# Nineteen weight slots instead of fifteen in the expert stage of a transformer layer, paid for with single row buffers and a residual that is stored and read back

## What is computed

```python
h = rms_norm(x, p['g_pre_ffn']) * (1 + sc) + sh
xb = t[tok_b]
hb = jax.nn.silu(xb @ w1[e]) * (xb @ w3[e])
return (hb @ w2[e]) * w_b[:, None]
...
return x + gt * rms_norm(hierarchical_moe(h, p), p['g_post_ffn'])
```

## Time and profile before

| | |
|---|---|
| median of 3 runs | 1144.94 us (1143.33 to 1145.46) |
| the profiled execution | 1144.4 us, of which the span of the trace is 1142.7 us |
| TensorE busy | 1004.3 us, 88% of the span |
| VectorE, ScalarE, GpSimd busy | 355.0, 280.8, 138.3 us |
| DMA queue of SP | 271.07 MB, 60.5% of the 16 engines' span |
| HBM read, written | 283.34 MB, 25.33 MB |

### The profile page before, as it was taken

How to read it: one execution, slowest core, us unless ns; L and a number is a source line. 1 busy time by engine, 2 the same in 40 slices (tenths; PEclk the granted TensorE clock), 3 DMA queues, 4 the chain that set the end, 5 groups by cost and what they waited for, 6 DMA issues and landing times. The chain is left out here.

```text
span 1142.7 us, 13820 instructions
## 1 busy us (share of the span) xinstructions
PE 1004.3 (88%) x5483; PEld 606.3 (53%) x5483; DVE 355.0 (31%) x633; ACT 280.8 (25%) x533; POOL 138.3 (12%) x219
## 2 busy tenths in 40 slices
PE   4999999999988898999968997799999978588776
PEld 2677778777766787887854332233333322122222
DVE  3553133110388885462392110000000000000006
ACT  4233213222377664022341000000011000000004
POOL 2122221000111301100122000000001000000000
PEclk9899999999989999999997998899999998889999
DMA  9734436444350212633458999999999999999973
GB/s 350 254 113 160 126 110 226 160 168 177 123 184 1 77 55 66 230 129 93 184 202 283 369 401 420 421 422 421 421 420 420 421 419 419 419 416 413 416 312 135
DMA packets 73334, 301.55 MB, mean 264 GB/s; under 512 B 8055, under 2 KB 14328, under 8 KB 48050
## 3 DMA queue, kind: packets, MB, share of 16 engines
q1 hardware_dynamic: 62064, 271.07, 60.5%
q0 software_dynamic: 11040, 29.49, 7.6%
q10 hardware_dynamic: 162, 0.05, 0.0%
HBM read 283.34 MB, written 25.33 MB: 270 GB/s over the span
## 5 line engine op out<-in xcount | busy, mean ns | idle before, releaser
L1387 PE MATMUL psum<-w_hi,act_hi 128*128 128x512 f32 (+1 forms) x480 | 188.6, 393 | 2.8 <-ACT rows L1174 1.4
L1389 PE MATMUL psum<-w_hi,act_lo 128*128 128x512 f32 (+1 forms) x480 | 183.9, 383 | 0.0
L1388 PE MATMUL psum<-w_lo,act_hi 128*128 128x512 f32 (+1 forms) x480 | 183.7, 383 | 0.0
L1782 PE MATMUL psum<-weights_ring,expert_x_columns 128*64 128x512 f32 (+1 forms) x584 | 125.3, 634 | 29.5 <-DMA weights_ring<-in_w_e 18.5
L1320 ACT ACTIVATE expert_y<-psum 128x512 f32<-128x512 f32 x18 | 10.8, 597 | 455.3 <-PE psum L1793 455.3
L1782 PE MATMUL psum<-rows_ring,expert_x_columns 128*64 128x512 f32 (+1 forms) x448 | 103.6, 611 | 9.5 <-DMA rows_ring<-in_w_e 5.9
L1387 PEld LDWEIGHTS psum<-w_hi,act_hi 128*128 128x128 f32 x480 | 90.9, 189 | 32.4 <-issue 14.2
L1389 PEld LDWEIGHTS psum<-w_hi,act_lo 128*128 128x128 f32 x480 | 90.9, 189 | 18.2
L1388 PEld LDWEIGHTS psum<-w_lo,act_hi 128*128 128x128 f32 x480 | 91.1, 190 | 16.3
L1911 DVE TENSOR_TENSOR w_lo<-raw_mix,w_hi 128x2048 fp32r<-128x2048 f32 (+1 forms) x24 | 52.8, 2202 | 148.1 <-ACT w_hi L1069 148.1
L1782 PEld LDWEIGHTS psum<-weights_ring,expert_x_columns 128*64 128x64 f32 (+1 forms) x584 | 37.5, 136 | 103.5 <-issue 102.3
(11 more groups left out here) (345 smaller groups left out, 1275.2 us busy)
## 6 DMA issues: line engine op xcount, KB each, us to landing
weights_ring<-in_w_e SPq DMA_DIRECT2D x78, 1024.0 KB, 28.1
rows_ring<-in_w_e SPq DMA_DIRECT2D x75, 1024.0 KB, 28.5
raw_mix<-in_w_e SPq DMA_DIRECT2D x39, 1024.0 KB, 27.7
raw_mix<-in_w_in SPq DMA_DIRECT2D x16, 1024.0 KB, 5.8
raw_mix<-in_w_ada SPq DMA_DIRECT2D x16, 1024.0 KB, 7.1
ada_first<-in_w_ada SPq DMA_DIRECT2D x8, 1024.0 KB, 14.3
gates_scratch<-rows POOLq DMA_DIRECT2D x20, 256.0 KB, 3.3
y_scratch<-lam SPq DMA_DIRECT2D x1, 5120.0 KB, 16.8
```

What stands on the lines that cost most here:

```text
L1387: pe.matmul(out, a_hi(ka_), w_hi[:, kw, :], start=s, stop=False)
L1388: pe.matmul(out, a_hi(ka_), w_lo[:, kw, :], start=False, stop=False)
L1389: ins = pe.matmul(out, a_lo(ka_), w_hi[:, kw, :], start=False, stop=e)
L1782: ins = pe.matmul(out[x * w:(x + 1) * w, :], expert_xT[:, a:a + w], ring(slots[x % len(slots)])[:, kk * 512:(kk + 1) * 512], start=(k == 0 ...
```

## The change

The ring has 19 slots. Four more are gained by laying the rows ring over 80 KB per partition that end at the tile `pt`. These lie over x1 too, so x1 is stored to HBM (`x1_d`) and read back at the end into ring slots, half a slot per tile (`x1_back`). `xg` and `ysb` have one half instead of two, and the gather of pass p then waits for the transposes of pass p-1, the copy of pass p's result for the scatter of pass p-1. The loads are sorted so that the 12 of passes 0 and 1 go first, and loads 9 to 12 are issued singly, each as its slot comes free.

```diff
-RAW_MIX, RING, HL = 3, 15, 3
+RAW_MIX, RING, HL = 3, 19, 3
...
+    loads.sort(key=lambda x: x[1] >= LEAD)
+    return units, loads + [(len(units), len(passes), 0, i, 0) for i in range(NT + (NT + 1) // 2)]
...
+        xg = at("expert_rows", D, offset=late_base + 2 * D * 4)
+        ysb = at("expert_y", D, offset=late_base + 3 * D * 4)
...
+        rows_ring_base = pt_base - (RING - RAW_MIX - 2 * HL) * UNIT * 4
...
+            x = [9, 0, 6, 7, 1, 2, 8, 5, 4, 3][slot - RAW_MIX - 2 * HL]
...
+        def x1_back(i):
+            return ring((PAIR_LOAD + NT + i // 2) % RING)[:, i % 2 * D:(i % 2 + 1) * D]
...
             def load_pair(i):
                 sp.dma_start(raw_pair(i), y_d[2 * P * i:2 * P * (i + 1), :].rearrange("(p k) n -> p (k n)", k=2)).then_inc(x_in[i], 16)
+                sp.dma_start(x1_back(i), x1_d[i * P:(i + 1) * P, :]).then_inc(x_in[i], 16)
...
                     ring_load(RAW_MIX + 2 * x + 1)
+                    if x == 0:
+                        ring_load(9)
+                ring_load(10)
+                for i in range(NT):
+                    if i == NT - 1:
+                        sp.wait_ge(mix_done, 6 * NT)
+                        ring_load(11)
+                    sp.wait_ge(x1_done, i + 1)
+                    sp.dma_start(x1_d[i * P:(i + 1) * P, :], xrow[:, i, :]).then_inc(h2_out, 16)
                 for i in range(NT):
                     sp.wait_ge(h2_done, i + 1)
                     sp.dma_start(h2_d[i * P:(i + 1) * P, :], yr[:, i, :]).then_inc(h2_out, 16)
-                sp.wait_ge(h2_out, 16 * NT)
+                sp.wait_ge(h2_part, NT)
+                ring_load(12)
+                sp.wait_ge(h2_out, 32 * NT)
                 sp.wait_ge(h2t_done, 2 * NT)
...
             def first_part(i, again):
-                ac.wait_ge(x_in[i], 32 + 16 * again)
+                ac.wait_ge(x_in[i], 48 + 32 * again)
...
-                ve.scalar_tensor_tensor(raw_pair(i)[:, 0:D], raw_pair(i)[:, D:2 * D], stat[:, 8 + i:9 + i], xrow[:, i, :], ALU.mult, ALU.add).then_inc(c_out, 1)
+                ve.scalar_tensor_tensor(raw_pair(i)[:, 0:D], raw_pair(i)[:, D:2 * D], stat[:, 8 + i:9 + i], x1_back(i), ALU.mult, ALU.add).then_inc(c_out, 1)
```

More of the change, by code:

```diff
@@ L106, in expert_units @@
     loads = [(n, p, m, u, x) for n, (p, m, u) in enumerate(units) for x in range(len(passes[p]))]
-    return units, loads + [(len(units), len(passes), 0, i, 0) for i in range(NT)]
+    loads.sort(key=lambda x: x[1] >= LEAD)
+    return units, loads + [(len(units), len(passes), 0, i, 0) for i in range(NT + (NT + 1) // 2)]
 def build(nc, t):
@@ L264, in build @@
         idx_s = at("scatter_column", 2, U32)
-        rbase = [late_base + 4 * D * 4]
+        rbase = [late_base + 3 * D * 4]
         def rb(name, cols, dt=F32):
@@ L270, in rb @@
             rbase[0] += (cols * (2 if dt == BF16 else 4) + 31) // 32 * 32
-            assert rbase[0] <= late_base + 6 * D * 4
+            assert rbase[0] <= late_base + 4 * D * 4 + FE * 4
             return a
-        kbase = [late_base + 7 * D * 4 + FE * 4]
+        kbase = [late_base + 5 * D * 4 + FE * 4]
         def kept(name, cols, dt=F32):
@@ L278, in kept @@
             kbase[0] += (cols * (2 if dt == BF16 else 4) + 31) // 32 * 32
-            assert kbase[0] <= late_base + 2 * KD * TOK * 4
+            assert kbase[0] <= rows_ring_base
             return a
@@ L336, in ring @@
                 return weights_ring[:, x * UNIT:(x + 1) * UNIT]
-            x = slot - RAW_MIX - 2 * HL
+            x = [9, 0, 6, 7, 1, 2, 8, 5, 4, 3][slot - RAW_MIX - 2 * HL]
             return rows_ring[:, x * UNIT:(x + 1) * UNIT]
@@ L475, in build @@
         h2_done = sem("h2_rows_done")
-        h2_out = sem("h2_stored")
+        h2_out = sem("x1_and_h2_stored")
         h2t_done = sem("h2_transposed")
@@ L754, in all_experts @@
                     sp.dma_start(h2_d[i * P:(i + 1) * P, :], yr[:, i, :]).then_inc(h2_out, 16)
-                sp.wait_ge(h2_out, 16 * NT)
+                sp.wait_ge(h2_part, NT)
+                ring_load(12)
+                sp.wait_ge(h2_out, 32 * NT)
                 sp.wait_ge(h2t_done, 2 * NT)
-                for j in range(RAW_MIX + 2 * HL, len(moe_loads)):
-                    if j == RAW_MIX + 2 * HL + 4:
-                        sp.wait_ge(moe_g[0], 16)
-                    if j == RING - 1:
-                        sp.wait_ge(rt_mm, 1 + NT)
+                for j in range(13, len(moe_loads)):
                     ring_load(j)
@@ L771, in pairs @@
             def pairs(again):
+                if not again:
+                    sp.wait_ge(moe_mm, moe_loads[PAIR_LOAD + NT + (NT - 1) // 2 - RING][0] + 1)
+                    sp.wait_ge(all_scattered, 1)
                 for i in range(NT):
-                    if again:
-                        load_pair(i)
+                    load_pair(i)
                 for i in range(NT):
@@ L965, in _ @@
             last_row, last_pair = po.to_reg(TOK - 1), po.to_reg(2 * TOK - 1)
-            po.wait_ge(h2_out, 16 * NT)
+            po.wait_ge(h2_out, 32 * NT)
             def gather(p):
-                if p >= 2:
-                    po.wait_ge(moe_xt, p - 1)
+                if p >= 1:
+                    po.wait_ge(moe_xt, p)
                 if p == LEAD:
@@ L998, in _ @@
             gather(0)
-            gather(1)
             po.wait_ge(tile_mm, 5 * NS)
@@ L1005, in _ @@
             po.dma_start(wk_d.rearrange("(t p k) o -> p t (k o)", p=P, k=2), wk[:, :].rearrange("p (t k) -> p t k", k=2)).then_inc(g2_in, 16)
+            gather(1)
             for p in range(NP - 1):
@@ L1039, in _ @@
                 for i in range(NT):
-                    po.wait_ge(x_in[i], 32)
+                    po.wait_ge(x_in[i], 48)
                 scatter(NP - 1)
@@ L1317, in y_half @@
                 ac.wait_ge(moe_mm, unit_end(p, 2, 1))
-                if p >= 2:
-                    ac.wait_ge(moe_sc[par], 16 * (p // 2))
-                ac.activation(ysb[:, par * D:par * D + 512], bank(5), ACT.Copy).then_inc(moe_ya, 1)
+                if p:
+                    ac.wait_ge(moe_sc[1 - par], 16 * ((p + 1) // 2))
+                ac.activation(ysb[:, 0:512], bank(5), ACT.Copy).then_inc(moe_ya, 1)
             def first_part(i, again):
-                ac.wait_ge(x_in[i], 32 + 16 * again)
+                ac.wait_ge(x_in[i], 48 + 32 * again)
                 if not again and i == 0:
@@ L1814, in transpose_x @@
                     pe.wait_ge(moe_xc, p)
-                rows_transposed(p % 2).then_inc(moe_xt, 1)
+                rows_transposed().then_inc(moe_xt, 1)
             def pair_rows(i):
@@ L1860, in _ @@
                 for x in range(2):
-                    pe.matmul(bank(SUM_BANK[i] + x), loh[:, i * P:(i + 1) * P], ysb[:, LAST_PAR * D + x * 512:LAST_PAR * D + x * 512 + 512], start=True, stop=False)
+                    pe.matmul(bank(SUM_BANK[i] + x), loh[:, i * P:(i + 1) * P], ysb[:, x * 512:x * 512 + 512], start=True, stop=False)
                 pair_rows(i)
@@ L2376, in y_half @@
                 ve.wait_ge(moe_mm, unit_end(p, 2, 1))
-                if p >= 2:
-                    ve.wait_ge(moe_sc[par], 16 * (p // 2))
-                ve.tensor_copy(ysb[:, par * D + 512:(par + 1) * D], bank(6)).then_inc(moe_yv, 1)
+                if p:
+                    ve.wait_ge(moe_sc[1 - par], 16 * ((p + 1) // 2))
+                ve.tensor_copy(ysb[:, 512:D], bank(6)).then_inc(moe_yv, 1)
             ve.wait_ge(pass_mm, 3)
@@ L2386, in pair_sum @@
             def pair_sum(i, again):
[L2387 removed]
+                ve.wait_ge(x_in[i], 48 + 32 * again)
                 ve.wait_ge(c_part, NT * again + i + 1)
```

34 lines of the change are left out of this document (14 added, 20 removed).

## The result

| | us, median (lowest to highest) | executions |
|---|---|---|
| before | 1143.85 (1142.05 to 1145.46) | 10 |
| changed | 1150.09 (1146.92 to 1154.33) | 10 |

The ratio is 1.0053, 95% interval 1.0040 to 1.0067: slower by half a per cent, clear of the spread, and outside the forecast range of 1141.8 to 1149.5 us. The profiled execution took 1150.62 us, its span is 1148.7 us.

What follows compares the result with a forecast made beforehand. The expert stage was taken as bound by weight transfers, the end by the last weight load's landing and the tail: -4.5 + 5.2 = +0.7 us, 1145.1 us profiled, 1145.6 us on the median, range 1141.8 to 1149.5 us.

Steps and rivals of the forecast that it cites:

- Part 2: Tail: x1 read back alternately with the result pairs delays the fourth tile's first part by 5.2 us (5.0 to 6.0).
- The spacing: Tail: one result pair plus its x1 transfer lands every 3.7 to 4.0 us.
- `first_part(4)` adds nothing: Tail: the last tile's data land 18.9 us after the last weight load; ScalarE arrives at 18.8 us, so no added delay.
- Three loads are worth 7.5 us: Front, at load 29's issue: three loads outstanding before, an empty queue now, a gain of 7.5 us before refilling costs.
- I take 4.5 us: Front: both queues full after load 30, so the last weight load lands 4.5 us earlier (4.2 to 5.1).
- The filling: Front: with an empty queue load 29 lands 4.9 us after issue instead of 2.5 us, costing 2.4 us.
- Load 30: Front: the load after 29 lands at 671.3 us instead of 675.5 to 677.6 us, at least 4.2 us gained.
- Hidden by 0.4 us at worst: Front: the second gather lands at 615.8 to 620.5 us, before TensorE wants its rows at 620.9 us; no cost.
- TensorE starts late: Rival, front: late h2 stores or second gather delay TensorE 2 to 4 us, giving 1147.6 to 1149.6 us; chance 0.25.
- The front gains nothing: Rival, front: load 29 late or engines slow for another reason, only the tail's loss left, 1150.1 us; chance 0.08.
- load 29 waits for the same unit of TensorE in both kernels: Front: load 29 reuses the slot of the same weight half in both kernels, so is issued at 662.9 us in both.
- my bound of 600.8 us: Front: the last h2 store lands at most 6.5 us later, at 600.8 us, hidden by 1.2 us before the first gather.

Runs made afterwards that it cites:

- the kernel before with the trip of x1: The kernel before, its slots, load order and buffers kept, with x1 stored and read back alternating with the result pairs: 1149.71 us, ratio 1.0045.
- unit order: The changed kernel with ring slots taken by later loads in the order in which TensorE's units free them: 1141.25 us, ratio 0.9988.
- the early gather: The changed kernel with the second gather issued right behind the first, ahead of the small transfers: 1146.54 us, ratio 1.0023.

## Why the prediction was wrong

**Tail: the mechanism was right, the size off.** Part 2 had 5.2 us, at most 6.0 us; it measured 6.2 us in the changed kernel and 6.3 us alone. The spacing was right (3.70 us, forecast 3.7 to 4.0) and `pair_root(0)` came 5.1 us later against L. The missing term is what the idle stretch does to TensorE: 5.7 us without work, then products at half the clock, 1.1 us at the end. Its size varies with how long the low clock lasts. In the five profiles with the alternation the two groups of four products behind the idle stretch took 3.58 + 1.88, 3.78 + 2.12, 3.78 + 1.94, 3.78 + 2.61 and 3.78 + 2.69 us, and the tails were 38.6, 39.1, 39.2, 39.5 and 39.6 us. `first_part(4)` adds nothing, as forecast: its x1 landed at 1127.94 us, ScalarE came to it at 1127.96 us.

**Front: the step that failed is "Three loads are worth 7.5 us", and with it "From there on both queues are full and L moves by the same amount. I take 4.5 us."** Load 29 was issued 52.3 us behind the first product as forecast when the gather was in time, and the queue was empty then. But three loads not landed are not three loads still to be moved. By the time load 29 is issued, the kernel before with the trip of x1 and the changed kernel with x1 behind the pairs have issued the same transfers; what the first has moved less is what still stands in its queue. Their windows (from 60 us before the first product to the issue of load 29, then the 15 us behind it), the kernel before with the trip first:

```profile
549.75:662.05 112.30, 98.19 (x555) 57.74 (x555) 47.83 (x105) 24.50 (x47) 20.30 (x21) 0.91 0.83 305
662.05:677.05 15.00, 15.00 (x90) 5.03 (x86) 3.18 (x9) 2.10 (x3) 2.02 (x2) 1.00 0.99 407
...
549.99:662.29 112.30, 98.14 (x555) 57.72 (x555) 47.53 (x105) 24.52 (x47) 19.45 (x21) 0.91 0.83 324
662.29:677.29 15.00, 15.00 (x88) 4.98 (x84) 3.18 (x9) 2.10 (x3) 2.02 (x2) 1.00 0.92 342
```

The second is ahead by (324 - 305) x 112.3/419 = 5.1 us of transfer, not 7.5 us, and then loses (407 - 342) x 15/419 = 2.3 us in filling, where I had 2.4 us. So 5.1 - 2.3 = 2.8 us are left, which is what L shows (496.0 against 498.8 us). The filling was right, the worth of the three loads was not. Load 30 hid this: it lands at 665.8 + 5.3 = 671.1 us, 61.1 us behind the first product against 65.5 us before, 4.4 us, as forecast. But load 31 lands 5.0 us earlier, 32 3.8, 34 3.2, 40 2.7 and the last 2.8 us: one landing does not measure what the 16 engines have moved.

**"Hidden by 0.4 us at worst" fell too.** The bound was 11.0 us, the slowest of 16 gathers. The second gather took 11.8 us in the first profile and 10.9 us in the second, 10.6 us being what it had; already gathers 2 to 17 of the changed kernel take up to 11.2 us. Where it was late by 1.2 us it took away nearly all of the 2.8 us. This was my rival "TensorE starts late" (0.25), with a delay of 2.7 us at load 29; that rival's 1147.6 to 1149.6 us missed the clock in the tail and took 4.5 us as the front's gain. My rival "The front gains nothing" (0.08) names a late load 29 among its conditions and 1150.1 us as its time, which is the measured median. That it fits so closely is luck: its tail was 1.0 us too short, and in the second profile of the same kernel the front did gain 2.5 us. That this gather is exposed at all comes from the single row buffer: before it had landed at 609.4 us, 1.2 us before the first product. The Trainium skill's page "Trainium Kernel Development and Optimization" (Best Practices) says "Double-buffer for performance". I weighed it by the 16 later passes, where the single buffer does cost nothing (419 GB/s from 670 to 1085 us, as before), and not by the second gather, which has 10.6 us to hide in.

**What I saw and did not read.** The prediction says that load 29 waits for the same unit of TensorE in both kernels, with four slots more. That is not a neutral fact: it means that the four new slots bring nothing to load 29. In sorted order the slot rule `j - RING` no longer follows the order in which slots are freed. By that rule the front gains at most 2.8 us, by the order of the units 8.9 us (498.8 to 489.9 us). With x1 behind the pairs, so that the tail costs nothing, that is nearly all of the time: 1134.50 us, 8.4 us under the kernel before of the same executions.

**h2 stores.** In the changed profile they landed 10.1 to 12.7 us after issue, the last at 601.9 us, 1.1 us beyond my bound of 600.8 us, and still 0.2 us ahead of the table. The first gather was issued 0.2 us later than before, the first product came at 610.6 us in both. The cover held, barely.

**The sum, redone:** 1144.4 - 0.1 + 6.2 = 1150.5 us for the profiled execution, which took 1150.6 us. In the profiles with the old slot rule the front gains 0.1 us (gather 1.2 us late, clock lower behind it), 2.5 us (0.3 us late) and 2.8 us (in time, three profiles). The medians do not follow the profiles closer than some 1.4 us, in both directions. Putting x1 behind the pairs took off 6.75 us on unit order (1141.25 to 1134.50), where a late gather no longer moves L (489.9 us with it and without) and the tails differ by 5.4 us; with the early gather it took off 4.7 us (1146.54 to 1141.85) where the tails differ by 5.8 us. The length of the low clock, which differs from profile to profile, is part of this; the rest is open. One reading of a row was off by one: from slice 24 to 37 the row has 413 to 422 GB/s, not 412 to 423, which changes nothing.

## What to carry to other kernels

When loads are sorted, sort the slots that they take too: a load should take the slot that comes free first, not the one that lies a fixed number of loads back. Where a queue is the bound, ask at each wait whether anything is still queued when it ends, and place transfers that wait for nothing ahead of one that waits (3.5 us of L here). What an emptied queue is worth is counted in bytes still to be moved, not in loads not yet landed. Among transfers that end the kernel, put what the last step reads behind what the first step reads: here 6 us for a reordering without a byte less.

## What was not expected of the hardware

- TensorE idle for 5.70 us in the tail: granted clock 0.78 in the stretch, 0.50 behind it, four products of 128x512 in 3.78 us instead of 1.98 us. Idle for 1.02 us ahead of the second transposes, where it had not been idle before: granted clock 0.52 in the two microseconds behind it, eight transposes in 1.97 us instead of 1.16 us. Idle for 0.78 us in the same place with unit order alone: granted clock 1.00, eight transposes in 1.16 us.
- One and the same gather of 128 rows took from 8.9 to 11.8 us over twelve profiles with weight transfers under way at its issue, and 5.0 and 5.8 us in the kernel before and with the x1 trip, where it was issued some 4 us ahead of them. The less the engines moved in the five microseconds behind its issue (415 down to 219 GB/s), the longer it took, on the whole.
- A window with the 16 engines busy all the time (share 1.05) moved 237 GB/s while the store of the pair weights (5 KB in pieces of 8 bytes) came to its end among weight transfers, against 411 and 420 GB/s in the same window without it; 2.5 us of it moved 80 GB/s.
- After ten microseconds at 155 and 87 GB/s the engines moved 341 GB/s in the next five, where the same windows without the hole had 397, 401 and 411.
